# Second mixer: where the spatial products stand between the down products on TensorE

## The reference

```python
def mixer_b(h, w_in, b_in, ln_g, ln_b, w_sp, b_sp, w_out):
    z = jax.nn.gelu(h @ w_in + b_in)
    u, v = jnp.split(z, 2, axis=-1)
    v = layernorm(v, ln_g, ln_b)
    ...
    w = jnp.where(tri[None], w_sp, jnp.zeros((), w_sp.dtype))
    sv = jnp.einsum('gts,bcsgd->bctgd', w, v) + jnp.transpose(b_sp)[None, None, :, :, None]
    y = u * sv.reshape(B_, S, B_HALF)
    return y @ w_out
```

## Time and profile before

| | |
|---|---|
| median of 3 runs | 1361.87 us (1361.49 to 1361.95) |
| profiled execution | 1361.84 us, span of the core 1359.9 us |
| PE busy | 1351.5 us (99%) |
| DVE, ACT, POOL busy | 939.2, 674.7, 49.7 us |
| DMA | 260.07 MB, 191 GB/s on average |
| stage `mixb` | roughly from 1030 to 1170 us of the span |

### The profile page before, as it was taken

One profiled execution on the slowest core, in us unless ns is written; L12 is line 12 of the kernel. 1 busy time (PEld: TensorE's weight loads), 2 busy tenths in 40 slices (PEclk: granted clock), 3 DMA queues, 4 the chain that ended last, 5 costly groups with the idle time before them and its releaser, 6 DMA issues. The chain is left out here.

```text
span 1359.9 us, 18452 instructions
## 1 busy us (share of the span) xinstructions
PE 1351.5 (99%) x7481; PEld 1173.6 (86%) x7481; DVE 939.2 (69%) x1106; ACT 674.7 (50%) x842; POOL 49.7 (4%) x77
## 2 busy tenths in 40 slices
PE   9999999999999999999999999999999999999998
PEld 8888888898888899888888888888888888888886
DVE  7777556776666778866666766666768877676665
ACT  6525434364444542654444554445554444554443
POOL 1010000020000100020000000000000000000000
PEclk9999999999999999999999999999999999999999
DMA  8638464545555473346454454455473555465540
GB/s 317 252 134 308 152 242 155 217 147 225 189 197 195 147 263 125 124 171 248 186 186 186 155 217 186 186 188 215 161 272 120 218 205 200 155 229 199 192 155 31
DMA packets 38483, 260.07 MB, mean 191 GB/s; under 512 B 4449, under 2 KB 4625, under 8 KB 8705
## 3 DMA queue, kind: packets, MB, share of 16 engines
q1 hardware_dynamic: 34848, 244.50, 48.4%
q0 software_dynamic: 3552, 14.40, 3.0%
HBM read 257.81 MB, written 2.64 MB: 192 GB/s over the span
## 5 line engine op out<-in xcount | busy, mean ns | idle before, releaser
L820 DVE TENSOR_TENSOR wlo<-raw,whi 128x2048 fp32r<-128x2048 f32 x228 | 519.9, 2288 | 72.7 <-ACT whi L539 72.5
L539 ACT ACTIVATE whi<-raw 128x2048 fp32r<-128x2048 f32 x228 | 433.8, 1909 | 34.6 <-DMA raw<-slabs_dram 26.7
L1386 PE MATMUL acc<-whi,ht 128*128 128x512 f32 x544 | 214.2, 394 | 0.0
L1387 PE MATMUL acc<-wlo,ht 128*128 128x512 f32 x544 | 212.4, 390 | 0.0
L1388 PE MATMUL acc<-whi,ht 128*128 128x512 f32 x544 | 211.9, 389 | 0.0
L1615 PE MATMUL mm<-xt,whi 128*128 128x512 f32 x848 | 201.5, 390 | 0.0
L1615 PE MATMUL tp<-xt,whi 128*128 128x512 f32 x848 | 201.4, 390 | 0.0
L1615 PEld LDWEIGHTS tp<-xt,whi 128*128 128x128 f32 x848 | 158.5, 188 | 33.2 <-DVE hid L935 0.6
L1615 PEld LDWEIGHTS mm<-xt,whi 128*128 128x128 f32 x848 | 158.7, 188 | 33.0 <-DVE hid L935 0.3
L935 DVE TENSOR_TENSOR hid<-mm,hid 128x512 f32<-128x512 f32 x58 | 40.1, 691 | 190.9 <-ACT hid L602 190.9
L602 ACT ACTIVATE hid<-mm 128x512 f32<-128x512 f32 x58 | 34.6, 597 | 265.3 <-PE mm L1622 255.6
(11 more groups left out here) (249 smaller groups left out, 1602.5 us busy)
## 6 DMA issues: line engine op xcount, KB each, us to landing
raw<-slabs_dram SPq DMA_DIRECT2D x228, 1024.0 KB, 4.9
vec<-vectors_dram POOLq DMA_DIRECT2D x12, 512.0 KB, 5.4
raw<-first_dram SPq DMA_DIRECT2D x8, 384.0 KB, 5.6
tables_dram<-table_dram POOLq DMA_DIRECT2D x1, 1536.0 KB, 9.3
hlf<-slabs_dram SPq DMA_DIRECT2D x1, 1024.0 KB, 7.8
vec<-forget_dram POOLq DMA_DIRECT2D x1, 1024.0 KB, 9.3
h<-x_dram POOLq DMA_DIRECT2D x2, 512.0 KB, 6.1
htf<-tables_dram POOLq DMA_DIRECT2D x1, 1024.0 KB, 8.8
```

The lines of the kernel that those rows point to most:

```text
L539: nc.scalar.activation(whi[:, m % RING, :], raw[:, m % RAW, :], ACT.Copy).then_inc(hi_done, 1)
L820: nc.vector.tensor_tensor(wlo[:, m % RING, :], raw[:, m % RAW, :], whi[:, m % RING, :], ALU.subtract).then_inc(lo_done, 1)
L1386: nc.tensor.matmul(out, a[0], b[0], start=first, stop=False)
L1387: nc.tensor.matmul(out, a[0], b[1], start=False, stop=False)
```

## The change

The calls of `spatial` move within PE's program. The first chunk's sets and spatial(1, 0) stay. spatial(1, 1) is issued behind up(2, 0). From chunk 2 on both sets of a chunk are issued behind tile q = 2 of the downs before it.

```diff
--- before.py
+++ after.py
@@ -1704,8 +1704,11 @@
                                     ins = down(c, q, t, half)
                         if i == 1:
                             ins.then_inc(slab_used, 1)
-                        if stg is mixb and q == 2 * i + (c == 0):
-                            spatial(c + 1, i)
+                        if stg is mixb and (c, q) == (0, 1):
+                            spatial(1, 0)
+                        if stg is mixb and c > 0 and q == 2:
+                            spatial(c + 1, 0)
+                            spatial(c + 1, 1)
 
                 def tail_by_half():
 
@@ -1786,6 +1789,8 @@
                     if stg is mixb and c == 1:
 
                         pe.wait_ge(stg.hid_ready, 2)
+                    if stg is mixb and c == 2:
+                        spatial(1, 1)
                     if c < last or (by_half and not f.gated):
                         downs(c - 1, 0)
                     up(c, 1)
```

## The result

The changed kernel takes 1386.75 us in the median of 5 runs (1386.01 to 1387.77), the kernel before 1361.74 (5 runs): a ratio of 1.0184, 95% interval 1.0173 to 1.0195, or 25.0 us more. Forecast were 1384.3 us and a range of 1379.8 to 1390.0.

What follows compares the result with a forecast made beforehand. TensorE, busy 1351.5 of 1359.9 us, was taken as the bound, so its delays are paid nearly in full. To 1361.84 us came 19.1 for waits and small terms and 3.4 for clock: 1384.3 us, range 1379.8 to 1390.0.

Steps and rivals of the forecast that it cites:

- the clock term: TensorE's clock falls behind one or two of the four new waits: 3.4 us, with ends of 0 and 8.4 us.
- The chain: Second set waits for DVE's L935, behind work needing the first set: 5.29 us for c = 2 to 4, 3.85 for c = 5.
- the signs: Expected in the profile after: four PE waits for L935, set distances 6.1 three times and 4.7, a chunk 29 us.
- The moved set at no cost: Moving spatial(1, 1) from behind q3 to behind up(2, 0) costs nothing by itself.
- The old wait and the steps between kinds of products: On PE: wait ahead of spatial(2, 0) removed, -0.63 us; waiting sets' steps +0.27; one step saved per pair, -0.3.
- the rival *faster: Second set finds unit (c, 1) already taken, saving 4 x 0.08 and the old wait's 0.72: 1360.8 us; 2%.
- Who is late next: Behind the waits, slab splits arrive in time; the tail's q2 needs P + 6.2 against P + 6.4: 0, or 0.3 us.
- the forecast case: The four waits plus a clock loss in one or two of them: 1382.5 to 1386.5 us; 34%.
- the case of all or nearly all waits: Rival: the clock falls in all or nearly all of the four waits, up to 1389.3 us and a little more; 20%.
- No clock loss: Rival: the four waits come without any clock loss, 1380.9 us; 30%.
- Second shortage: Rival: splits start late and q0 waits for its slab too; one split late three times gives 1391 us; 7%.
- shorter chain: Rival: the chain between the sets is shorter, 3 us less per wait, 1370 to 1378 us; 6%.

Runs made afterwards that it cites:

- filler run: Changed kernel with unused extra matmuls between the two sets of each pair, 20 for c = 2 to 4 and 14 for c = 5: 1381.64 us.
- reordered queues: Changed kernel with DVE and ACT evacuating unit (c, 1) first from chunk 2 on: 1363.09 us; with the last chunk's split behind unit (5, 1) as well: 1361.60 us.
- pairs alone: Changed kernel with spatial(1, 1) back at its old place behind q3, both later sets still behind q2: 1386.68 us.
- short filler: Changed kernel with 6 unused extra matmuls between the sets for c = 2 to 4 and none for c = 5: 1388.04 us.
- late `normalize_v`: Changed kernel with normalize_v of unit (c, 0) moved behind unit (c, 1), for c from 2: 1385.34 us.
- the moved set: Kernel before with only spatial(1, 1) moved behind up(2, 0), all later sets at their old places: 1364.62 us.

## Why the prediction was right

*The sum.* Forecast were 1384.3 us, measured are 1386.75. The waits and small terms were forecast at 19.1 us and came to 19.0; the clock term was 3.4 and came to 6.0, and the second term is the whole miss.

*What bounds the kernel.* Right: the mixer takes 25.0 us longer, and 19.0 of them are PE's waits less the small terms, 6.0 its slower products. PE has no new wait for anything but L935.

*The chain.* Right to 0.01 us, since the trace of before held it once complete at its only wait. The distances between the sets were 6.10, 6.09, 6.10 and 4.65 us, forecast 6.09 three times and 4.65. The filler run measures the term by itself: 19.6 us, forecast 19.1. The reordered queues remove it entirely. A chunk took 31.4 and 31.0 us and not the 29 of the signs, which left the clock out.

*The moved set at no cost.* Right for the whole change (pairs alone: 1386.68 against 1386.75, and 0.01 us in the profiles). Alone it costs 1.8 us in the profile, which the same reading gave for it.

*The old wait and the steps between kinds of products.* The wait is gone, as forecast, and its 0.7 us with it (0.7 in the profile with the first set behind q1). The +0.09 and -0.08 of each pair nearly cancel. The chunk from 1082.24 to 1113.63 takes 31.39 us, where 23.83 + 5.30 + 2.27 and these two give 31.41. But where the second set need not wait (reordered queues) it starts 0.89 behind the first all the same, so the 0.08 a pair that the rival *faster* counted on is not to be had.

*Who is late next.* Right: no wait for a slab or for `ht` in the mixer. How thin the margin of 0.2 us in the tail was, the run with the reordered queues shows: with unit (5, 1) behind a split there, PE waited 1.6 us for its low part.

*The clock.* The mechanism was right, the size too small. I took 3.4 us, a loss in one or two of four waits; the profile shows three, 6.0 us together. The term was mis-sized because I had only two rows far from the new waits and went between them. What the runs put in its place: 6.0 us in the profile, about 5 by the filler run, and a loss that does not follow the length of the wait. That each loss came out close to the 2.1 us of the opening is in part luck. The view of windows has a granted clock of 1.00 over the opening's slow products, in both kernels, and they stand 0.49 us apart where those under 0.50 in the mixer stand 0.43. That the opening was slow for the same reason is not shown.

*The range.* The measured time lies 0.25 us above the 1382.5 to 1386.5 of the forecast case, which had 34%, and inside the case of all or nearly all waits, which had 20%. The range holds it because both ends of the clock term had been kept open, not because the term was well placed.

*The Trainium skill's rule* ("TensorE: Matmul & The Clock Gate", section "HAM oscillation — how this bites in real kernels", that waits between groups of matmuls throttle the array again and again). The runs agree: the granted clock fell to 0.50 at three of four waits, and at all four in three other kernels (pairs alone, short filler, late `normalize_v`).

*The rivals.* No clock loss: needs 1380.9, that is the filler run and not this kernel. Clock lost in all four: it happens in those three, and the times alone can't tell it from three. The five executions of the changed kernel had mean granted clocks of 0.992 to 0.995, the profiled one 0.992, so the others need not have lost it at the same three waits. Second shortage, shorter chain, faster: none seen. (The recorded 1370 to 1378 for a shorter chain is a rough sum: 3 us less at each of four waits is 1372.3, and 1368.9 without the clock.)

*What stays open.* When exactly the clock falls, and for how long. In the profiled executions, standstills of 2.3 us lost it in two of three cases, two of four, and not in the single one of the moved set; standstills of 3.6 us lost it nine times in ten; those of 5.05 us six times in six.

## What to carry to other kernels

When a change puts two producers behind each other in one queue, ask whether the second needs something that stands behind the *first's consumer* in another engine's queue. If it does, the work that used to lie between them was hiding a whole round trip, and the trace often holds that round trip already at some small wait, where its length can be read off. The cure is to keep work between the two, as the kernel before does, or to let the consuming engine free the second one's buffer ahead of its work on the first (1361.60 us with the pairs kept). And on TensorE a round trip can cost more than its length: here 5 to 6 us of clock on 19 us of waits.

## What was not expected of the hardware

The clock falls after shorter standstills than I had thought of: waits of 2.3 us lost some 1.5 us each in four of eight profiled cases, about two thirds of their own length again. The fall can come late: behind one wait of 3.6 us, 1.5 us of products ran at full pace before the half pace began, so the slow stretch need not touch the wait ahead of it. It can also come early, inside the wait, and then a part of it is free: in the changed kernel the granted clock fell 2.0, 2.7 and 3.0 us ahead of the end of its three waits, was 0.50 for 6.8 us each time, and cost 2.27, 1.94 and 1.82 us. So shorter waits were no cheaper: 3.6 us cost up to 2.9 us of clock in one kernel and none once in another. Extra matmuls that filled all but 0.4 to 0.5 us of each wait kept the clock at 1.00.
